# Pooling's mixing products moved between the token tiles of the last v chunk, their split moved to GpSimd

## The chip, the cores and the metric

The kernel is one program on one core of a Trainium2 chip. The metric is device time in microseconds: the median of three executions. One further execution was taken with the hardware profiler, and every row below comes from it. Engines are named as the profile names them: PE is TensorE, DVE is VectorE, ACT is ScalarE, POOL is GpSimd, SP issues DMAs.

## What is computed

Two blocks follow each other on 256 tokens of width 1024. The first, a two-layer transformer block with a context of 256 more tokens, holds the change. In each of its layers a projection makes u, q, k and v; u goes through a pooling mixer and q, k, v through differential attention, and both results side by side go through `w_out`:

```
u, q, k, v = split_heads(h @ w_in[l])
...
y = jnp.stack([centred_mean(g, w) - g for g, w in zip(groups, POOL_WINDOWS)], axis=2)
y = jnp.einsum('bngc,gcd->bngd', y, w_pool).reshape(b, n, POOL_WIDTH)
return y * s_pool
...
s = jnp.einsum('bhqd,bhkd->bhqk', q, k).astype(jnp.float32) * (HEAD_DIM ** -0.5)
a = jax.nn.softmax(s, axis=-1).reshape(b, N_HEADS, 2, nq, nk)
w = a[:, :, 0] - lam * a[:, :, 1]
return jnp.einsum('bhqk,bhkd->bhqd', w.astype(v.dtype), v)
...
mix = jnp.concatenate([pool_mixer(u, w_pool[l], s_pool[l]), head_out(o_att, g_subln[l], lam_init)], axis=-1)
x = x + ga * (mix @ w_out[l])
```

There are four pooling groups of 128 channels. The einsum with `w_pool` is what the code calls a mixing product, or mix. Layer 0 works on 512 tokens (context and latent), layer 1 attends over 512 keys but needs its results for 256 tokens only. The second block (another attention, a recurrence, feed-forward parts) is not touched.

## The kernel before

All large matrix products are made of three products each, because weights and activations are held as a rounded high part and a low remainder: `w_hi` and `w_lo`, `h_hi` and `h_lo`. Weights come in chunks of 1 MB, numbered through the whole program (`N_WIN[l]` is the first chunk of layer l's input projection, `N_WOUT[l]` the first of its output projection). For a chunk, ACT makes `w_hi` (`split_hi`), and DVE, or for a few chunks POOL (`weight_lo`), makes `w_lo`, each in two halves.

The engines run without a scheduler: each has its own instruction stream in the order in which the code is written, and semaphores tie the streams together. So a waiting instruction holds up everything behind it on its engine.

The input projection of a layer has eight chunks, c = 0 to 7. The last, c = 7, holds half of v and is computed by `gemm_t` in four token tiles of 128 tokens, 24 products each, one after the other. Its result lies in PSUM banks 2 and 3; DVE copies it to `v_tok` and then counts `psum_free` up. `score(l, 0)`, the scores of the first attention unit, stands before c = 7, and DVE and ACT make that unit's weights while c = 7 runs.

Attention follows, in units: 16 in layer 0 (the first eight over 512 keys, the other eight over 256), 8 in layer 1 (all over 512 keys). For a unit i, PE makes `score(l, i)`, two products (L798); DVE finds the maxima (L2001) and scales them (`maxima`, L2003); ACT exponentiates (L1438); DVE takes the reciprocals of the sums (L2012), a small factor (L2014) and the weights `wgt` from the two halves of `prob` (`weights`, L2018); PE transposes `wgt` into bank 0 (L810); ACT copies that to `wgtT` (L1446, `copyT`); PE multiplies by `v_tok` (`values`, L820). PE's stream in a unit is transposes(i), score(i + 3), values(i). Banks for scores alternate over 4-5, 6-7 and 2-3, so `score(l, 2)` has to wait until c = 7 has been copied out of banks 2 and 3.

Pooling sits in between. POOL makes `pool_y` from u during the projection (`centred`). The four mixes (`pool_mix`, L788) are issued by PE at the start of attention, mingled with scores 1 and 2; ACT writes their rounded high part to `h_hi` (`pool_hi`, L1429), DVE the remainder to `h_lo` (`pool_lo`, L1993). In banks 1, 4, 5 and 1 (`MIX_BANK`) these results lie where later scores and values go, so PE waits for `po_lo` three times:

```
pe.wait_ge(po_lo, 4 * l + 1)
pool_mix(l, 3)
pe.wait_ge(po_lo, 4 * l + 3)
...
if i == 0:
    pe.wait_ge(po_lo, 4 * l + 4)
```

POOL's part at that time is `weight_lo(N_WOUT[l] + 1, ...)`, two instructions on 128x1024 elements. `h_hi` and `h_lo` are also the operands of c = 7, so nothing may be written to them before c = 7 ends.

Of the kernel before, what the change touches and what calls it, by code (L numbers as in the profile page):

```python
# [99 lines left out]
def build_program(nc, w_stream, w_ada, x_in, vec_in, cst_in, pool_inv, gla_masks, gla_sums, w_pool, w_gk, w_gk2,  # L100
                  out):
    ctx = ExitStack()
    with ctx:
# [116 lines left out]
        def sem(name):  # L220
# [27 lines left out]
        y_ready, po_done, po_hi, po_lo = (  # L248
            sem("y_ready"), sem("po_done"), sem("po_hi"), sem("po_lo"))
# [92 lines left out]
        MIX_BANK = (1, 4, 5, 1)  # L342
# [72 lines left out]
        def _(pool):  # L415
# [48 lines left out]

            for i in range(ADA_WIN):
# [7 lines left out]
                if i in (3, 5, 7, 9):  # L473
                    centred(0, (i - 3) // 2)
            weight_lo(N_WOUT[0] + 1, 0)
# [23 lines left out]
            for g in range(4):  # L499
                centred(1, g)  # L500
            weight_lo(N_WOUT[1] + 1, 0)
# [47 lines left out]
        def _(pe):  # L549
# [123 lines left out]
            def gemm_t(n, tiles, ready=None, bank=None, free=None, middle=None):  # L673
# [6 lines left out]
                for i in range(tiles):  # L680
# [10 lines left out]
                    if i == 0 and middle is not None:  # L691
                        middle()
                last.then_inc(gemm_done, 1)
# [90 lines left out]
            def pool_mix(l, g):  # L784

                w = ALLT if l == 0 else SEQ
                pe.wait_ge(y_ready, 4 * l + g + 1)
                mm(ps[:, MIX_BANK[g], 0:w], wp[:, l, g, :], pool_y[:, g, 0:w], start=True, stop=True).then_inc(po_done, 1)  # L788

# [12 lines left out]
            def attention(units, u0, q0, l):  # L802
# [51 lines left out]
                if l == 0:  # L854
                    ada_columns(4, 4)
                transposes(0)
                pe.wait_ge(pool_in, 32)
                pool_mix(l, 0)
                pool_mix(l, 1)
                pe.wait_ge(ada_ready, 3 + 6 * l)  # L860
                score(l, 1)
                pool_mix(l, 2)
                pe.wait_ge(psum_free, N_WIN[l] + 8)
                score(l, 2)
                pe.wait_ge(po_lo, 4 * l + 1)
                pool_mix(l, 3)
                pe.wait_ge(po_lo, 4 * l + 3)
                for i in range(count):
# [118 lines left out]
            for l in range(2):  # L987
                n0 = N_WIN[l]
                hr = (h_ready, H0[f"win{l}"])
                for c in range(8):  # L990
# [5 lines left out]
                    elif c < 6:  # L996
                        gemm_f(n, h_hi, h_lo, slice(0, ALLT if l == 0 else SEQ), None, bank=bank, free=free)
                    else:
                        gemm_t(n, 4, bank=bank, free=free)
# [331 lines left out]
        def _(act):  # L1331
# [93 lines left out]
            def pool_hi(l, g):  # L1425
# [1444 lines left out]
```

## Time and profile before

| what | value |
|---|---|
| runs, median (lowest to highest) | 1576.99 us (1576.82 to 1578.64) |
| the profiled execution's own time | 1578.42 us |
| span of its records | 1576.6 us |
| PE busy | 1550.2 us, 98% |
| DVE busy | 1102.3 us, 70% |
| ACT busy | 744.1 us, 47% |
| POOL busy | 162.4 us, 10% |
| mean granted clock of TensorE | 0.995 |
| c = 7 of layer 0 ends, its attention begins | at 134.8 us of the span |
| c = 7 of layer 1 ends, its attention begins | at 676.6 us of the span |

Times inside the run are microseconds from the start of the span. A line of a timeline gives when a group of like instructions started and how long it took, and in brackets how long the engine had been idle and for whom it waited. A mean clock of 1.00 is 2.4 GHz, 0.50 is 1.2 GHz. Two fp32 products of this kernel are two records of PE each, so a count x4 stands for two products.

### The profile page before, as it was taken

The numbers are of one execution on the slowest core, as the hardware profiler recorded it, in microseconds if no ns is written. First come the engines' busy times: TensorE is split into PE (matmuls) and PEld (weight loads), VectorE is DVE, ScalarE is ACT, GpSimd is POOL, SyncE is SP. The second block draws the span as 40 slices with busy tenths as digits, with TensorE's granted clock in tenths as the row PEclk, the third lists the DMA queues.
The fourth block names the chain that finished last, engine by engine and source line by source line (L and its number), as shares of the span: only waits on it lengthen the run. The fifth ranks groups of instructions, "written<-read, shape, count | busy, mean of one in ns | idle before, by whom it ended". The sixth has DMA issues, their size and how long they took to land.

```text
span 1576.6 us, 27327 instructions
## 1 busy us (share of the span) xinstructions
PE 1550.2 (98%) x11138; PEld 1403.2 (89%) x11138; DVE 1102.3 (70%) x1674; ACT 744.1 (47%) x1064; POOL 162.4 (10%) x151
## 2 busy tenths in 40 slices
PE   9999999999999999999999999999999999999998
PEld 6786777888888887978999999999999999999998
DVE  5676658555565666867666678668786889887786
ACT  4215534222231323355444465667464567665554
POOL 0341100000000000410000010201020211021110
PEclk9999999999999999999999999999999999999999
DMA  9861453432343432415544543335455445545541
GB/s 391 327 239 58 175 198 110 159 108 105 134 159 122 144 117 84 171 69 194 191 180 162 211 159 108 117 138 178 183 187 188 161 164 184 188 161 205 178 181 52
DMA packets 36525, 257.76 MB, mean 163 GB/s; under 512 B 4087, under 2 KB 4088, under 8 KB 5968
## 3 DMA queue, kind: packets, MB, share of 16 engines
q1 hardware_dynamic: 29952, 211.85, 37.0%
q0 software_dynamic: 6480, 44.58, 7.4%
q8 instruction: 69, 1.13, 0.3%
q14 instruction: 24, 0.20, 0.0%
HBM read 255.37 MB, written 1.05 MB: 163 GB/s over the span
## 4 chain that ended last, share of the span: by engine, by line
PE 87%; DVE 6%; ACT 4%; issue 2%; DMA 2%; SPq 0%; DVEq 0%; ACTq 0%
PE ps L578 17%; PE ps L580 17%; PE ps L579 17%; PE ps L616 4%; PE ps L615 4%; PE ps L614 4%; PE ps L702 1%; PE ps L686 1%; PE ps L595 1%; PE ps L820 1%; PE ps L597 1%; PE ps L596 1%; PE ps L687 1%; PE ps L688 1%; DVE w_lo L1866 1%
## 5 line engine op out<-in xcount | busy, mean ns | idle before, releaser
L1351 ACT ACTIVATE w_hi<-w_raw 128x1024 fp32r<-128x1024 f32 x378 | 395.7, 1056 | 526.6 <-PE ps L580 300.7
L1866 DVE TENSOR_TENSOR w_lo<-w_raw,w_hi 128x1024 fp32r<-128x1024 f32 x375 | 468.4, 1253 | 142.0 <-ACT w_hi L1351 138.5
L578 PE MATMUL ps<-h_hi,w_hi 128*128 128x256 f32 (+1 forms) x1616 | 496.0, 307 | 0.7 <-DVE h_lo L1919 0.3
L580 PE MATMUL ps<-h_hi,w_lo 128*128 128x256 f32 (+1 forms) x1616 | 493.1, 305 | 0.0
L579 PE MATMUL ps<-h_lo,w_hi 128*128 128x256 f32 (+1 forms) x1616 | 493.0, 305 | 0.0
L578 PEld LDWEIGHTS ps<-h_hi,w_hi 128*128 128x128 f32 x1616 | 308.7, 191 | 18.0 <-issue 2.7
L580 PEld LDWEIGHTS ps<-h_hi,w_lo 128*128 128x128 f32 x1616 | 308.7, 191 | 13.4
L579 PEld LDWEIGHTS ps<-h_lo,w_hi 128*128 128x128 f32 x1616 | 308.8, 191 | 12.8
L614 PE MATMUL ps<-g_hi,w_hi 128*128 128x256 f32 (+1 forms) x448 | 140.4, 313 | 0.0
L615 PE MATMUL ps<-g_lo,w_hi 128*128 128x256 f32 (+1 forms) x448 | 140.4, 313 | 0.0
L616 PE MATMUL ps<-g_hi,w_lo 128*128 128x256 f32 (+1 forms) x448 | 140.4, 313 | 0.0
L2087 DVE SCALAR_TENSOR_TENSOR x<-ps,ada,x 128x256 f32<-128x256 f32 x120 | 50.9, 477 | 90.2 <-PE ps L616 60.3
L578 PE MATMUL ps<-g_hi,w_hi 128*128 128x256 f32 (+1 forms) x368 | 111.4, 303 | 0.0
L580 PE MATMUL ps<-g_hi,w_lo 128*128 128x256 f32 (+1 forms) x368 | 111.0, 302 | 0.0
L579 PE MATMUL ps<-g_lo,w_hi 128*128 128x256 f32 (+1 forms) x368 | 110.9, 301 | 0.0
L2568 DVE SCALAR_TENSOR_TENSOR conv_y<-ffn_s,vec,conv_y 128x255 f32<-128x255 f32 x192 | 95.6, 539 | 7.6 <-ACT conv_y L1744 5.7
L614 PEld LDWEIGHTS ps<-g_hi,w_hi 128*128 128x128 f32 x448 | 85.5, 191 | 5.0
L615 PEld LDWEIGHTS ps<-g_lo,w_hi 128*128 128x128 f32 x448 | 85.5, 191 | 5.0
L616 PEld LDWEIGHTS ps<-g_hi,w_lo 128*128 128x128 f32 x448 | 85.5, 191 | 5.0
L2334 DVE TENSOR_TENSOR relu<-relu 128x1024 f32<-128x1024 f32 (+1 forms) x32 | 30.7, 959 | 69.7 <-ACT relu L1565 69.7
L580 PEld LDWEIGHTS ps<-g_hi,w_lo 128*128 128x128 f32 x368 | 70.4, 191 | 2.6
L579 PEld LDWEIGHTS ps<-g_lo,w_hi 128*128 128x128 f32 x368 | 70.4, 191 | 2.4
(375 smaller groups left out, 2505.0 us busy)
## 6 DMA issues: line engine op xcount, KB each, us to landing
w_raw<-in_w_stream SPq DMA_DIRECT2D x188, 1024.0 KB, 4.8
ada_r<-in_w_ada POOLq DMA_DIRECT2D x20, 1024.0 KB, 5.2
ada_g<-in_w_ada POOLq DMA_DIRECT2D x16, 1024.0 KB, 7.5
ada_r<-in_w_ada SPq DMA_DIRECT2D x4, 1024.0 KB, 14.2
ada_g<-in_w_ada SPq DMA_DIRECT2D x4, 1024.0 KB, 22.8
ada_s<-in_w_ada POOLq DMA_DIRECT2D x4, 1024.0 KB, 5.2
x<-in_x_in SPq DMA_DIRECT2D x2, 1024.0 KB, 6.2
w_raw<-in_w_stream SPq DMA_DIRECT2D x4, 512.0 KB, 18.4
```

Source lines behind the costliest of these rows:

```text
L578: mm(o, wh, hi[:, k, cols], start=(k == 0), stop=False)
L579: mm(o, wh, lo[:, k, cols], start=False, stop=False)
L580: last = mm(o, wl, hi[:, k, cols], start=False, stop=(k == KT - 1))
L595: mm(o, wh, hi[:, k, cols], start=(k == 0), stop=False)
L614: mm(o, wh, hi[:, k, cols], start=(k == 0), stop=False)
L615: mm(o, wh, lo[:, k, cols], start=False, stop=False)
L616: last = mm(o, wl, hi[:, k, cols], start=False, stop=(k == KT - 1))
L1351: A(w_hi[:, n % 2, k, :].rearrange("p k n -> p (k n)"), w_raw[:, n % 4, k.start * CH:k.stop * CH], ACT.Copy)\
L1866: TT(w_lo[:, n % 2, k, :].rearrange("p k n -> p (k n)"), w_raw[:, n % 4, k.start * CH:k.stop * CH], w_hi[:, n % 2, k, :].rearrange("p k n ...
L2087: last = STT(x[:, t, c], ps[:, bank + m, c], ada[:, l, part + t, s:s + 1], x[:, t, c], ALU.mult, ALU.add)
L2334: TT(relu2[:, :, 0:w], relu[:, c % 2, :, 0:w], relu[:, c % 2, :, 0:w], ALU.mult)\
L2568: last = STT(y, ffn_s[:, t, 0:SEQ - back], V(f"ffn{l}", o), y, ALU.mult, ALU.add)
```

## The change

In both layers the same things are moved. PE: the four mixes leave the start of attention and go behind the first token tile of c = 7 (mixes 0 and 1, in layer 0 also `ada_columns(4, 4)`) and behind the second (mixes 2 and 3); `score(l, 1)` and the transposes of unit 0 go behind the third. The waits of PE for `po_lo` at the start of attention are gone; one remains before the first product of `w_out`. Mixes now lie in banks 7, 1, 0 and 7. ACT: the two-step split is replaced by one plain copy of each mix into `pool_y` (`mixed_copy`), ahead of the exponentials of unit 1; those and `copyT` of unit 0 now stand ahead of the `split_hi` that follows c = 7. POOL: `mixed_split` waits until c = 7 has ended, then makes `h_hi` by a copy and `h_lo` by a subtraction for each group, and only then comes its `weight_lo`. DVE: the four `pool_lo` are gone, and `maxima(l, 1)` (and `ada_columns` in layer 0) go ahead of the copy of v. ACT's copies of `o_raw`, which lies over `pool_y`, wait for `po_lo`.

```diff
-        MIX_BANK = (1, 4, 5, 1)
+        MIX_BANK = (7, 1, 0, 7)
...
+            def mixed_split(l):
+
+                w = ALLT if l == 0 else SEQ
+                pool.wait_ge(gemm_done, N_WIN[l] + 8)
+                for g in range(4):
+                    pool.wait_ge(po_copied, 4 * l + g + 1)
+                    own.step(nc.gpsimd.tensor_copy(h_hi[:, g, 0:w], pool_y[:, g, 0:w]))
+                    own.join()
+                    PT(h_lo[:, g, 0:w], pool_y[:, g, 0:w], h_hi[:, g, 0:w].bitcast(F32), ALU.subtract).then_inc(po_lo, 1)
...
+            mixed_split(0)
...
+            mixed_split(1)
...
+                    if i in between:
+                        between[i]()
...
             def pool_mix(l, g):
                 w = ALLT if l == 0 else SEQ
+                if l == 0 and g == 0:
+                    pe.wait_ge(pool_in, 32)
+                if g == 1:
+                    pe.wait_ge(psum_free, N_WIN[l] + 7)
+                if g == 3:
+                    pe.wait_ge(po_copied, 4 * l + 1)
                 pe.wait_ge(y_ready, 4 * l + g + 1)
                 mm(ps[:, MIX_BANK[g], 0:w], wp[:, l, g, :], pool_y[:, g, 0:w], start=True, stop=True).then_inc(po_done, 1)
+
+            def mixes(l, pair):
+
+                if l == 0 and pair == 0:
+                    ada_columns(4, 4)
+                pool_mix(l, 2 * pair)
+                pool_mix(l, 2 * pair + 1)
+
+            def first_units(l):
+
+                u, kb = 16 * l, (ALLT - UNITS[l][0][2]) // P
+                pe.wait_ge(po_copied, 4 * l + 4)
+                pe.wait_ge(ada_ready, 3 + 6 * l)
+                score(l, 1)
+                pe.wait_ge(wgt_ready, u + 1)
+                for b in range(kb):
+                    last = nc.tensor.transpose(ps[:, 0, b * P:(b + 1) * P], wgt[:, u % 2, b * P:(b + 1) * P], ident)
+                last.then_inc(wgtT_done, 1)
...
-                if l == 0:
-                    ada_columns(4, 4)
-                transposes(0)
-                pe.wait_ge(pool_in, 32)
-                pool_mix(l, 0)
-                pool_mix(l, 1)
-                pe.wait_ge(ada_ready, 3 + 6 * l)
-                score(l, 1)
-                pool_mix(l, 2)
                 pe.wait_ge(psum_free, N_WIN[l] + 8)
                 score(l, 2)
-                pe.wait_ge(po_lo, 4 * l + 1)
-                pool_mix(l, 3)
-                pe.wait_ge(po_lo, 4 * l + 3)
...
+                            pe.wait_ge(po_lo, 4 * l + 4)
...
-                    if i == 0:
-                        pe.wait_ge(po_lo, 4 * l + 4)
...
+                        gemm_t(n, 4, bank=bank, free=free,
+                               between={0: lambda: mixes(l, 0), 1: lambda: mixes(l, 1), 2: lambda: first_units(l)})
...
-            def pool_hi(l, g):
+            def mixed_copy(l, g):
                 w = ALLT if l == 0 else SEQ
                 act.wait_ge(po_done, 4 * l + g + 1)
-                A(h_hi[:, g, 0:w], ps[:, MIX_BANK[g], 0:w], ACT.Copy, scale=V(f"s_pool{l}", g)).then_inc(po_hi, 1)
+                A(pool_y[:, g, 0:w], ps[:, MIX_BANK[g], 0:w], ACT.Copy, scale=V(f"s_pool{l}", g)).then_inc(po_copied, 1)
...
+                    act.wait_ge(po_lo, q + 1)
...
-                copyT(0)
-                pool_hi(l, 0)
-                pool_hi(l, 1)
-                exponentials(l, 1)
-                pool_hi(l, 2)
-                pool_hi(l, 3)
...
+                        for g in range(4):
+                            mixed_copy(l, g)
+                        exponentials(l, 1)
+                        copyT(UNITS[l], 16 * l, 0)
...
-            def pool_lo(l, g):
-
-                w = ALLT if l == 0 else SEQ
-                dve.wait_ge(po_hi, 4 * l + g + 1)
-                STT(h_lo[:, g, 0:w], ps[:, MIX_BANK[g], 0:w], V(f"s_pool{l}", g), h_hi[:, g, 0:w].bitcast(F32),
-                    ALU.mult, ALU.subtract).then_inc(po_lo, 1)
...
-                pool_lo(l, 0)
-                maxima(l, 1)
-                pool_lo(l, 1)
-                pool_lo(l, 2)
                 weights(l, 1)
-                pool_lo(l, 3)
...
                     else:
                         maxima(l, 0)
                         weights(l, 0)
+                        if l == 0:
+                            ada_columns(0, 4, 4, 32)
+                        maxima(l, 1)
```

PE's stream in layer 0, from the last product of c = 7 on, before (`cst,rows` is `ada_columns`, `cst,wgt` are transposes, `pool_y,wp` mixes, `kT,qT` scores, `v_tok,wgtT` values):

```order
L713 MATMUL ps<-cst,rows 128x8 x2
L810 MATMUL ps<-cst,wgt 128x128 x4
L788 MATMUL ps<-pool_y,wp 128x512 x2
L798 MATMUL ps<-kT,qT 128x512 x2
L788 MATMUL ps<-pool_y,wp 128x512
L798 MATMUL ps<-kT,qT 128x512 x2
L788 MATMUL ps<-pool_y,wp 128x512
L798 MATMUL ps<-kT,qT 128x512 x2
L820 MATMUL ps<-v_tok,wgtT 128x128 x4
```

PE's stream in layer 0 now; the rows with `h_hi,w_hi`, `h_lo,w_hi` and `h_hi,w_lo` are products of c = 7, and 24 of them stand between two of the inserted pieces:

```order
L727 MATMUL ps<-cst,rows 128x8 x2
L808 MATMUL ps<-pool_y,wp 128x512 x2
L698 MATMUL ps<-w_hi,h_hi 128x256
...
L700 MATMUL ps<-w_lo,h_hi 128x256
L808 MATMUL ps<-pool_y,wp 128x512 x2
L698 MATMUL ps<-w_hi,h_hi 128x256
...
L836 MATMUL ps<-kT,qT 128x512 x2
L825 MATMUL ps<-cst,wgt 128x128 x4
L698 MATMUL ps<-w_hi,h_hi 128x256
...
L700 MATMUL ps<-w_lo,h_hi 128x256
L836 MATMUL ps<-kT,qT 128x512 x4
L858 MATMUL ps<-v_tok,wgtT 128x128 x4
L848 MATMUL ps<-cst,wgt 128x128 x4
L836 MATMUL ps<-kT,qT 128x512 x2
```

All four mixes, one score and one set of transposes stand between products of c = 7, and behind its last product two scores and the values of unit 0 come at once.

POOL's stream in layer 0 from the end of `centred` on, before (two DMAs of other weights, then `weight_lo`):

```order
L462 TENSOR_TENSOR pool_y<-win_sum,u_pad 128x512
L468 DMA ada_g_72<-in_w_ada 128x2048
L468 DMA ada_g_73<-in_w_ada 128x2048
L428 TENSOR_TENSOR w_lo<-w_raw,w_hi 128x1024 x2
L481 DMA ada_r_68<-in_w_ada 128x2048
```

and now:

```order
L478 DMA ada_g_73<-in_w_ada 128x2048
L471 CAST h_hi<-pool_y 128x512
L473 TENSOR_TENSOR h_lo<-pool_y,h_hi 128x512
...
L471 CAST h_hi<-pool_y 128x512
L473 TENSOR_TENSOR h_lo<-pool_y,h_hi 128x512
L428 TENSOR_TENSOR w_lo<-w_raw,w_hi 128x1024 x2
L492 DMA ada_r_68<-in_w_ada 128x2048
```

Eight instructions on 128x512 elements have come between those DMAs and `weight_lo`; in layer 1 the same eight work on 128x256.

## Rows read from the trace of the kernel before

**Rows 1.** The page: busy time, share of the span and instructions of each engine.

```profile
PE 1550.2 (98%) x11138; PEld 1403.2 (89%) x11138; DVE 1102.3 (70%) x1674; ACT 744.1 (47%) x1064; POOL 162.4 (10%) x151
```

**Rows 2.** Windows: stretch, length, busy of PE PEld DVE ACT POOL, TensorE clock, DMA, GB/s.

```profile
144.00:150.00 6.00, 5.35 (x27) 3.66 (x26) 5.35 (x10) 3.27 (x9) 0.00 (x0) 0.72 0.00 0
676.00:690.00 14.00, 11.51 (x54) 6.81 (x53) 10.49 (x18) 8.21 (x20) 4.67 (x2) 0.88 0.20 76
```

**Rows 3.** Timeline of PE, layer 0: start, us, engine, line, operation, count, [idle before].

```profile
134.80 0.51 PE L713 MATMUL ps<-cst,rows 128*128 128x8 f32 x4
135.16 0.63 PE L810 MATMUL ps<-cst,wgt 128*128 128x128 f32 x4
135.63 1.88 PE L788 MATMUL ps<-pool_y,wp 128*128 128x512 f32 x4
137.45 1.13 PE L798 MATMUL ps<-kT,qT 64*128 64x512 f32 x4
...
142.95 1.13 PE L798 MATMUL ps<-kT,qT 64*128 64x512 f32 x4 [1.21 <-DVE h_lo L1993]
144.73 1.64 PE L820 MATMUL ps<-v_tok,wgtT 128*128 128x128 f32 x8 [0.65 <-DVE h_lo L1993]
...
149.93 0.60 PE L810 MATMUL ps<-cst,wgt 128*128 128x128 f32 x4
```

**Rows 4.** Timeline of PE, layer 1, the same columns.

```profile
676.60 0.60 PE L810 MATMUL ps<-cst,wgt 128*128 128x128 f32 x4
677.03 1.03 PE L788 MATMUL ps<-pool_y,wp 128*128 128x256 f32 x4
...
683.74 1.32 PE L798 MATMUL ps<-kT,qT 64*128 64x512 f32 x4 [2.30 <-DVE h_lo L1993]
...
690.12 0.60 PE L810 MATMUL ps<-cst,wgt 128*128 128x128 f32 x4
```

**Rows 5.** Timeline of DVE and PE in one unit of layer 1.

```profile
689.24 1.22 DVE L2001 TENSOR_REDUCE small<-ps 128x2 f32<-128x1024 f32 x1
...
690.50 0.17 DVE L2003 TENSOR_SCALAR small<-small 128x2 f32<-128x2 f32 x1
...
690.65 1.13 PE L798 MATMUL ps<-kT,qT 64*128 64x512 f32 x4
...
691.11 0.75 DVE L2018 SCALAR_TENSOR_TENSOR wgt<-prob,small 128x512 f32<-128x512 f32 x1
...
691.71 1.16 PE L820 MATMUL ps<-v_tok,wgtT 128*128 128x128 f32 x8
...
692.71 0.49 PE L810 MATMUL ps<-cst,wgt 128*128 128x128 f32 x3
```

**Rows 6.** Timeline of DVE, layer 0: the copy of the last v chunk.

```profile
135.00 1.23 DVE L2240 COPY v_tok<-ps 128x1024 f32<-128x1024 f32 x1 [7.03 <-PE ps L688]
```

**Rows 7.** Timeline of POOL, then its groups by form (busy us, mean ns).

```profile
60.08 1.30 POOL L462 TENSOR_TENSOR pool_y<-win_sum,u_pad 128x512 f32<-128x512 f32 x1
...
69.90 1.06 POOL L456 TENSOR_TENSOR win_sum<-u_pad 128x516 f32<-128x516 f32 x1
...
656.53 0.74 POOL L462 TENSOR_TENSOR pool_y<-win_sum,u_pad 128x256 f32<-128x256 f32 x1
...
L511 POOL MEMSET gq<- 128x1024 f32 x1 | 1.0, 957 | 20.2 <-DVE x L2087 20.2
```

**Rows 8.** Timeline of POOL and DVE where both work at once.

```profile
86.61 1.29 POOL L460 TENSOR_TENSOR win_sum<-win_sum,p_inv 128x512 f32<-128x512 f32 x1
...
86.67 1.78 DVE L1983 TENSOR_TENSOR qT<-qT,rope_tmp 128x512 f32<-128x512 f32 x1
...
87.98 1.63 POOL L462 TENSOR_TENSOR pool_y<-win_sum,u_pad 128x512 f32<-128x512 f32 x1
...
676.62 4.67 POOL L428 TENSOR_TENSOR w_lo<-w_raw,w_hi 128x1024 fp32r<-128x1024 f32 x2 [13.40 <-ACT w_hi L1351]
...
680.43 0.89 DVE L2003 TENSOR_SCALAR small<-small 128x2 f32<-128x2 f32 x1
```

More of the change, by code:

```diff
@@ L246, in build_program @@
         relu_ready, ghi_ready = sem("relu_ready"), sem("ghi_ready")
-        y_ready, po_done, po_hi, po_lo = (
-            sem("y_ready"), sem("po_done"), sem("po_hi"), sem("po_lo"))
+        y_ready, po_done, po_copied, po_lo = (
+            sem("y_ready"), sem("po_done"), sem("po_copied"), sem("po_lo"))
         qk_ready, pool_step = sem("qk_ready"), sem("pool_step")
@@ L671, in at_of, with gemm_t @@
                 return lambda k: ready[3] * ready[2] + (ready[1] + k)
-            def gemm_t(n, tiles, ready=None, bank=None, free=None, middle=None):
+            def gemm_t(n, tiles, ready=None, bank=None, free=None, middle=None, between=()):
                 start_chunk(n, same, free)
@@ L997, in _ @@
                         gemm_f(n, h_hi, h_lo, slice(0, ALLT if l == 0 else SEQ), None, bank=bank, free=free)
-                    else:
-                        gemm_t(n, 4, bank=bank, free=free)
+                    elif c == 6:
+                        gemm_t(n, 4, bank=bank, free=free)
+                    else:
+                        gemm_t(n, 4, bank=bank, free=free,
+                               between={0: lambda: mixes(l, 0), 1: lambda: mixes(l, 1), 2: lambda: first_units(l)})
                     if l == 0:
@@ L1423, in norm_split, with copyT @@
                         last.then_inc(norm_hi, 1)
-            def pool_hi(l, g):
+            def mixed_copy(l, g):
                 w = ALLT if l == 0 else SEQ
                 act.wait_ge(po_done, 4 * l + g + 1)
-                A(h_hi[:, g, 0:w], ps[:, MIX_BANK[g], 0:w], ACT.Copy, scale=V(f"s_pool{l}", g)).then_inc(po_hi, 1)
+                A(pool_y[:, g, 0:w], ps[:, MIX_BANK[g], 0:w], ACT.Copy, scale=V(f"s_pool{l}", g)).then_inc(po_copied, 1)
+            def copyT(units, u0, i):
+                u, w = u0 + i, ALLT - units[i][2]
+                act.wait_ge(wgtT_done, u + 1)
+                A(wgtT[:, u % 2, 0:w], ps[:, 0, 0:w], ACT.Copy).then_inc(wgtT_copied, 1)
             def exponentials(l, i):
@@ L1442, in attention @@
             def attention(units, u0, q0, l):
-                def copyT(i):
-                    u, w = u0 + i, ALLT - units[i][2]
-                    act.wait_ge(wgtT_done, u + 1)
-                    A(wgtT[:, u % 2, 0:w], ps[:, 0, 0:w], ACT.Copy).then_inc(wgtT_copied, 1)
                 def copy_o(q):
                     act.wait_ge(pv_done, u0 + 4 * (q - q0 + 1))
+                    act.wait_ge(po_lo, q + 1)
                     A(o_raw[:, q - q0, :], ps[:, 1, :], ACT.Copy).then_inc(o_copied, 1)
@@ L1477, in attention @@
                         A(sm(S_SQRT), sm(S_EPS), ACT.Sqrt)
-                    copyT(i)
+                    copyT(units, u0, i)
                     if i >= 4 and i % 4 == 0:
@@ L2249, in _ @@
                     if l == 0:
-                        if c in (3, 5, 7):
+                        if c in (3, 5):
                             ada_columns(0, (c + 1) // 2, 4, 4 * (c + 1))
```

## Prediction

> **What bounds the kernel now.** I read the page first: PE is busy for 98% of the span, DVE for 70%, POOL for 10% [rows 1]. So time can only be won in PE's idle and slow stretches, and at the start of attention there are both. I then went along PE's timeline in the two places. In layer 0 c = 7 ends at 134.80 and the transposes of unit 2 start at 149.93: 15.13 us, with two waits for `pool_lo` (1.21 and 0.65 us) [rows 3]. In layer 1 the same way goes from 676.60 to 690.12: 13.52 us, one wait of 2.30 [rows 4]. Last the windows: behind those waits the granted clock averages 0.72 over 6 us and 0.88 over 14 us, in both cases 3.4 us at the lower level (6 x 0.28 / 0.5 and 14 x 0.12 / 0.5) [rows 2]. The values of unit 0 take 1.64 us there, where the same eight records take 1.16 later [rows 3, 5].
>
> Behind that start PE takes 2.59 us for a unit: transposes at 690.12, score at 690.65, values at 691.71, the next transposes at 692.71, so 0.53, 1.06 and 1.00 [rows 4, 5]. DVE needs nearly as much: reduction to scaling 1.26 us, scaling to `wgt` 0.61, and 0.67 of `wgt`'s 0.75 (its end overlaps the next instruction), together 2.54 [rows 5]. PE is slower by 0.05 us a unit. A DVE that falls behind therefore takes PE with it, and nothing later in the units gives it back.
>
> **The change on PE.** Layer 0, by the rows: columns 0.36, two mixes 1.82 and again 1.82, a score 1.06, transposes 0.47 now stand inside c = 7 [rows 3, 5]: c = 7 ends 5.53 us later, at 140.33. ACT's copy of each pair of mixes has a token tile of c = 7 to hide behind, and of that tile's 24 products none waits for it. Then a new wait: `score(l, 2)` needs the copy of v, which DVE starts 0.20 us after c = 7 and which takes 1.23 [rows 6]; with 0.03 that I add for signalling PE idles 1.46 us, where mixes and scores covered this before. Queued behind it is all of PE's attention. Then two scores, values, transposes, score, values: 3 x 1.06 + 2 x 1.00 + 0.53 = 5.71. Transposes of unit 2 start at 140.33 + 1.46 + 5.71 = 147.50, which is 2.43 us earlier than 149.93. Layer 1: the four mixes are half as wide and take 0.96 a pair (1.03 less the overlap of its end) [rows 4], so 1.92 + 1.06 + 0.43 = 3.4 go into c = 7, which ends at 680.0; with the same 7.17 behind it the transposes of unit 2 start at 687.17, 2.95 earlier. The sum without POOL: **5.4 us gained**. It counts the full clock in both places; one wait of 1.46 is shorter than the 1.86 in two parts and the 2.30 that were followed by the low one.
>
> **The change on ACT and DVE, outside that.** ACT writes each mix once as before. Exponentials of unit 1 and `copyT` of unit 0 now precede the `split_hi` after c = 7; ACT idles for long stretches in c = 7 and is through some 2 us after its end, before it is needed for unit 2. DVE loses four `pool_lo`. The w_raw transfer that waits for `weight_lo` starts later and is for a chunk that comes after attention. I cost these at nothing; the cover is ACT's idle time in c = 7 and the 16 or 8 units before `w_out`.
>
> **The change on POOL.** POOL has work in attention, and this is the term that decides. Before, its two `weight_lo` (4.67 us, 2.34 each, [rows 8]) ran from the end of c = 7 while DVE worked on PSUM results. Now eight instructions precede them, and all ten run beside the first units. What that does to DVE the trace shows: a DVE instruction with two SBUF inputs that meets a running POOL instruction ends only after it. L1983 started at 86.67 beside a POOL instruction that ended at 87.90, and took 1.78 us, where L2018 of the same size takes 0.75 alone; the next POOL instruction took 1.63 instead of 1.30 in its turn [rows 5, 7, 8]. Even the scaling of two numbers, L2003, took 0.89 instead of 0.17 at 680.43, and ended with `weight_lo` at 681.3 [rows 5, 8]. The stretch is the rest of POOL's instruction less about 0.14. L2003, L2018 and the small L2014 between them are of this kind in every unit; the reduction reads PSUM alone and isn't. The v copy beside a running `weight_lo` took its 1.23 too [rows 6].
>
> The Trainium skill, page "SBUF — State Buffer", section "Who interferes with whom", has it as a rule: GpSimd shares a pair of SBUF ports with VectorE, an instruction takes it whole, and VectorE instructions with two SBUF inputs or in a 2-port mode contend, while a reduction never does. The trace agrees in each case above. By it the ten instructions cost time; a reading that counts POOL as idle capacity gives the 5.4 us gain.
>
> Durations for POOL: subtraction 1.30 us in layer 0 and 0.74 in layer 1, `weight_lo` 2.34 [rows 7, 8]. The SBUF copy is not in the trace: at least half of a memset of twice the size, 0.48, at most an addition with two inputs, 1.06 [rows 7]. I take 0.6 (0.35 in layer 1), since with one input it is nearer to the memset. The page "GPSIMD Engine Reference" of the Trainium skill, section "Engine selection", calls one-input operations roughly line-rate, which as an estimate would be about 0.45 us for 512 elements and 0.6 with its dispatch; the sum would be the same.
>
> Now step by step, in us after c = 7 of layer 0. POOL: copy 0.1 to 0.7, subtraction to 2.1, copy to 2.8, and so on. DVE: v copy to 1.35, reciprocal, L2014 meets the first subtraction (0.40 lost), `wgt` of unit 1 the second copy (0.36); scaling for unit 2 the third copy (0.43); `wgt` of unit 2 the fourth subtraction (0.16 and 1.07); scaling for unit 4 the first `weight_lo` (0.74); L2014 of unit 3 the second (2.08). Together 5.2 us; `wgt` of unit 3 is ready at 14.5 instead of 9.3. DVE has 0.4 us in hand, so the transposes of unit 3 are 4.8 us late, in idle stretches of about 1.0, 1.0 and 2.8. Layer 1, with the shorter instructions: 0.5 at unit 1, 0.1, then 1.9 and 2.1 at the two `weight_lo`: 4.5, and the transposes of unit 2 are 3.9 late. So without the clock layer 0 gives -2.43 + 4.8 = +2.35, layer 1 -2.95 + 3.9 = +0.95. The idle stretches are as long as those that the low clock followed before. 3.4 us at half the clock cost at most half of that, 1.7 us; part would be hidden by DVE's lag, so I add 1.0 in each layer. **Sum: 2.35 + 0.95 + 2.0 = +5.3 us.** The span of 1576.6 becomes 1581.9. The profiled execution's own time was 1578.42, 1.8 around its span and 1.4 above the median of the runs; with the same distances it becomes 1583.7, and the median 1576.99 + 5.3 = 1582.3.
>
> Bounds: with the copy anywhere from 0.48 to 1.06 the meetings shift, for whether a DVE instruction meets the start or the end of one of 2.34 us is chance. Layer 0 then lies between +2.1 and +5, layer 1 between 0 and +3; together +2.5 to +8. After `weight_lo` has ended (13.6 us after c = 7) nothing of this goes on, and its result is needed only after the units.
>
> **Rivals.**
>
> *Hidden anyway: faster.* POOL's turns cost PE nothing, because the units have slack that I don't see, or L2014 and L2018 don't take turns. Then the whole -5.4 stands, 1571.6 (1571 to 1573.5). For it: no L2018 met POOL before, so its own row is missing. Against: two other instructions with two SBUF inputs, and L2003 itself, did. It decides if PE's idle time behind the v copy stays under 1 us a layer. 0.21.
>
> *Half of it.* The two `weight_lo` fall beside reductions and waits for ACT, and only the short turns cost: in layer 0 the first five, 2.4 us, instead of 5.2, in layer 1 0.6 instead of 4.5, with no fall of the clock. Less 0.4 in hand in each that is -2.43 + 2.0 and -2.95 + 0.2, so -3.2; with one of the four long turns met after all about -1, and with one and a low stretch +1. I call it -3 to +2.5, with 1576.5 in the middle. For it: a reduction is 1.2 of DVE's 2.54 us. Against: a DVE instruction that waits for one `weight_lo` is there when the next begins. 0.20.
>
> *Slower, as worked out.* +2.5 to +8, likeliest 1582.3, its own range 1579.5 to 1585. 0.59.
>
> **How the numbers follow.** 0.2% (3.15 us) is about what a measurement of this kernel can tell from no change. The slower case passes +3.15 in nine of ten: 0.53, and a little more for a stall unseen: 0.56. Within 0.2%: the rest of it and most of the half case, 0.23. Faster: the hidden case, 0.21. The range is 1572.5 to 1586: it takes in both bounds of the likeliest, the half case, and a part of the hidden one.
>
> **What would show it.** In the profile after: mixes, score and transposes between products of c = 7 with no idle time ahead of them; PE idle about 1.4 us before the score of unit 2; the instructions of L2018 (now L2038) above their 0.75 us, up to 1.8, and those of L2014 (now L2034) up to 2.3, while POOL runs; POOL busy for 13 to 15 us after c = 7 in layer 0, 10 in layer 1; transposes of unit 3 of layer 0 about 14.5 us after c = 7. I am wrong if L2038 keeps 0.75 beside POOL, or if the waits ahead of PE are short although they are stretched.

## The result and the profile after

The changed kernel takes 1583.66 us (median of 5 executions, 1582.24 to 1584.21) against 1576.82 of the kernel before beside it: 1.0044 times as long, 95% interval 1.0033 to 1.0055, so 5.2 to 8.7 us slower. The forecast was 1582.3 us, 5.3 more than before. One of the twelve executions of a kernel below, the one with `weight_lo` shortened, took 2520.9 us at a mean granted clock of 0.554; the other eleven took 1573.40 to 1578.16, with a median of 1575.79.

The span of the profiled execution is 1579.9 us, only 3.3 above that of before. The rest of it is at the start of the program, which the change doesn't touch: c = 7 of layer 0 begins at 120.75 here and began 2.4 us later before (the last section comes back to it). I therefore compare stretches, which start with the first product of c = 7 and end with the last `values` of the layer. In the timeline of PE of the changed kernel, these rows bound layer 0:

```profile
120.75 0.39 PE L698 MATMUL ps<-w_hi,h_hi 128*128 128x256 f32 x1
...
178.08 0.71 PE L858 MATMUL ps<-v_tok,wgtT 128*128 128x128 f32 x4 [0.16 <-ACT wgtT L1462]
```

That is 178.79 - 120.75 = 58.04 us. Read in the same way, in us (the median of before is the one beside each group of kernels, and the ratios below are to that one):

| kernel | median | layer 0 | layer 1 | both, against before |
|---|---|---|---|---|
| before | 1576.5 to 1577.1 | 55.41 | 39.90 | |
| changed | 1583.66 | 58.04 | 43.08 | +5.8 |
| weight_lo shortened | 1575.98 | 55.19 | 37.29 | -2.8 |
| split shortened | 1575.64 | 54.68 | 38.17 | -2.5 |
| both shortened | 1572.84 | 53.30 | 36.83 | -5.2 |
| before, weight_lo shortened | 1575.90 | 54.93 | 38.61 | -1.8 |
| pieces behind reductions | 1575.22 | 55.30 | 37.37 | -2.6 |
| filler, too long | 1583.11 | 58.06 | 42.46 | +5.2 |
| filler, half | 1581.69 | 58.01 | 40.72 | +3.4 |
| weight_lo on VectorE | 1582.69 | 60.22 | 40.21 | +5.1 |
| split inside c = 7, pieces | 1572.57 | 53.42 | 36.84 | -5.1 |
| the same, weight_lo at once | 1581.78 | 56.98 | 42.83 | +4.5 |
| the same, pieces, two v copies | 1573.13 | 52.99 | 36.30 | -6.0 |

The stretches are read from one profiled execution of each kernel, and the medians don't agree with them in full: against before, each of the twelve kernels has a median 0.6 to 2.5 us higher than its stretches say. A part of this lies outside the span of the records: an execution's own time is longer than its span by 1.8 us in the kernel before, by 2.3 in the changed one and by 1.8 to 2.4 in the others. And the profiled execution of before had a low clock in both stretches [rows 2], which its others need not have had; there is no second trace of it. So against before the stretches make every kernel look better than its median does, by 1.2 us on average.

Now the stretch itself. The timeline of PE in the changed kernel answers to [rows 3, 4], layer 0 first, layer 1 from 681.73 on: L836 is the score, L848 the transposes, L858 the values.

```profile
137.76 0.28 PE L700 MATMUL ps<-w_lo,h_hi 128*128 128x256 f32 x1
139.35 1.99 PE L836 MATMUL ps<-kT,qT 64*128 64x512 f32 x8 [1.32 <-DVE v_tok L2258]
...
144.89 1.16 PE L858 MATMUL ps<-v_tok,wgtT 128*128 128x128 f32 x8 [0.96 <-ACT wgtT L1462]
146.71 1.07 PE L848 MATMUL ps<-cst,wgt 128*128 128x128 f32 x4 [0.66 <-DVE wgt L2038]
147.71 2.08 PE L836 MATMUL ps<-kT,qT 64*128 64x512 f32 x4
...
152.09 0.66 PE L848 MATMUL ps<-cst,wgt 128*128 128x128 f32 x4 [0.99 <-DVE wgt L2038]
...
681.73 1.99 PE L836 MATMUL ps<-kT,qT 64*128 64x512 f32 x8 [1.32 <-DVE v_tok L2258]
...
686.83 1.16 PE L858 MATMUL ps<-v_tok,wgtT 128*128 128x128 f32 x8 [0.53 <-ACT wgtT L1462]
691.12 1.11 PE L848 MATMUL ps<-cst,wgt 128*128 128x128 f32 x4 [3.14 <-DVE wgt L2038]
692.17 2.08 PE L836 MATMUL ps<-kT,qT 64*128 64x512 f32 x4
...
696.04 0.76 PE L848 MATMUL ps<-cst,wgt 128*128 128x128 f32 x4
```

The mixes are inside c = 7 without a wait, and the first score behind it waits 1.32 us for the v copy. The waits for `po_lo` are gone. In their place PE waits for `wgt` and `wgtT`: 0.96, 0.66 and 0.99 us in layer 0 and 0.53 and 3.14 in layer 1. From 146.71 and from 691.12 the same records take almost twice as long (1.07 and 2.08 us for 0.60 and 1.13). Why `wgt` is late stands in DVE's timeline, first of layer 0 and from 682.08 on of layer 1 (L2023 is the scaling, L2034 the small factor, L2038 `wgt`):

```profile
139.41 0.67 DVE L2034 SCALAR_TENSOR_TENSOR small<-small 128x1 f32<-128x1 f32 x1
140.12 1.05 DVE L2038 SCALAR_TENSOR_TENSOR wgt<-prob,small 128x512 f32<-128x512 f32 x1
...
142.34 0.54 DVE L2023 TENSOR_SCALAR small<-small 128x2 f32<-128x2 f32 x1
...
144.91 1.74 DVE L2038 SCALAR_TENSOR_TENSOR wgt<-prob,small 128x512 f32<-128x512 f32 x1
146.57 1.21 DVE L2021 TENSOR_REDUCE small<-ps 128x2 f32<-128x1024 f32 x1
147.82 1.06 DVE L2023 TENSOR_SCALAR small<-small 128x2 f32<-128x2 f32 x1
...
148.99 2.19 DVE L2034 SCALAR_TENSOR_TENSOR small<-small 128x1 f32<-128x1 f32 x1
...
682.08 1.30 DVE L2038 SCALAR_TENSOR_TENSOR wgt<-prob,small 128x512 f32<-128x512 f32 x1
...
685.97 1.96 DVE L2023 TENSOR_SCALAR small<-small 128x2 f32<-128x2 f32 x1
...
688.03 2.18 DVE L2034 SCALAR_TENSOR_TENSOR small<-small 128x1 f32<-128x1 f32 x1
```

And POOL's timeline of the changed kernel beside it:

```profile
138.10 0.61 POOL L471 CAST h_hi<-pool_y 128x512 fp32r<-128x512 f32 x1 [31.05 <-PE ps L700]
138.80 1.26 POOL L473 TENSOR_TENSOR h_lo<-pool_y,h_hi 128x512 fp32r<-128x512 f32 x1
...
146.06 5.10 POOL L428 TENSOR_TENSOR w_lo<-w_raw,w_hi 128x1024 fp32r<-128x1024 f32 x2
...
685.55 4.65 POOL L428 TENSOR_TENSOR w_lo<-w_raw,w_hi 128x1024 fp32r<-128x1024 f32 x2
```

In layer 0 the small factor of unit 3, one number a partition, starts at 148.99, soon after the second `weight_lo` has begun, and ends at 151.18, when that instruction ends (146.06 + 5.10 = 151.16). The reduction, which reads PSUM, keeps its 1.21 us beside POOL. The windows of the changed kernel (length, busy times, then the TensorE clock as the third number from the end) show the low level in both layers:

```profile
144.00:150.00 6.00, 4.45 (x17) 2.44 (x18) 5.59 (x8) 3.85 (x11) 5.92 (x5) 0.73 0.00 0
...
685.00:699.00 14.00, 10.34 (x49) 6.39 (x48) 11.79 (x16) 7.11 (x20) 5.20 (x3) 0.76 0.21 75
```

By the working of the prediction that is 6 x 0.27 / 0.5 = 3.2 us at 1.2 GHz in layer 0, as before, and 14 x 0.24 / 0.5 = 6.7 in layer 1, twice as much as before [rows 2].

### The profile page after: what moved, and what is told of

Same layout as the page of the kernel before. It is cut to its first block, busy times and chain, and to the rows that moved or that the text cites. A ratio compares the mean times of both kernels' runs of the same rounds, so it can differ in the third digit from the quotient of the medians.

```text
span 1579.9 us, 27342 instructions
## 1 busy us (share of the span) xinstructions
PE 1548.2 (98%) x11138; PEld 1403.4 (89%) x11138; DVE 1106.1 (70%) x1666; ACT 744.1 (47%) x1064; POOL 175.1 (11%) x167
## 3 DMA queue, kind: packets, MB, share of 16 engines
q8 instruction: 69, 1.13, 0.3%
## 4 chain that ended last, share of the span: by engine, by line
PE 86%; DVE 8%; ACT 3%; issue 2%; DMA 1%; SPq 0%; DVEq 0%; ACTq 0%
PE ps L590 17%; PE ps L591 17%; PE ps L592 17%; PE ps L628 4%; PE ps L627 4%; PE ps L626 4%; PE ps L716 1%; PE ps L698 1%; PE ps L607 1%; PE ps L609 1%; PE ps L608 1%; PE ps L700 1%; PE ps L699 1%; DVE w_lo L1893 1%; DMA ada_r<-in_w_ada 1%
```

## The experiments

My theory, called port theory below: a VectorE instruction with two SBUF inputs, or a scaling, that meets a running GpSimd instruction waits for it, and what waits for VectorE is PE; a low clock comes on top. Rivals: the new wait for the v copy is the cost, GpSimd's work costs wherever it stands, or the number of its instructions does.

**GpSimd's work cut away, one part at a time.** Three kernels from the changed one. The first leaves out all but 8 columns of each `weight_lo` of this chunk, the second all but 8 columns of each instruction of the split, the third both.

```diff
-                PT(w_lo[...], w_raw[...], w_hi[...], ALU.subtract)
+                e = 8 if cut else 1024
+                PT(w_lo[...][:, 0:e], w_raw[...][..., 0:e], w_hi[...][:, 0:e], ALU.subtract)
```
```diff
             def mixed_split(l):
-                w = ALLT if l == 0 else SEQ
+                w = 8
```

> The changed kernel with GpSimd's two weight_lo of each attention cut to 8 of their 1024 columns (the rest of that low part is left out), mixed_split as it is. Port theory (VectorE instructions with two SBUF inputs, or the scaling, wait for the running GpSimd instruction): in the changed kernel two VectorE instructions met each weight_lo pair, 1.06 + 2.19 us in layer 0 and 1.96 + 2.18 in layer 1 where 0.17 + 0.22 are normal. Without them 2.86 and 3.75 us go, and with layer 1's low clock behind its 3.14 us wait another 2 to 2.5: attention of both layers together 7 to 9 us shorter than in the changed kernel, so 1575 to 1577.5 us, with waits of about 1 us for the short turns still in layer 0. Rival, the new wait for the v copy (1.32 us) and the low clock after it are the cost and GpSimd's turns lie in slack: within 2 us of the changed kernel, 1582 to 1585.

> The changed kernel with mixed_split cut to 8 columns a piece (the split of the mixes is left out but for these), weight_lo as it is. It is short work then, so weight_lo starts about 1 us after the end of c = 7, when ScalarE has made w_hi, and ends near 5.7 us after it. Port theory: the long turns are still met by VectorE, now in unit 1 (small factor or weights, scaling), up to 2.2 us each; the short ones (0.45 + 0.30 + 0.37 + 0.99 us in layer 0, 0.04 + 0.55 + 0.09 in layer 1) are gone. Worked out along the stream: layer 0 1.5 us shorter than in the changed kernel, layer 1 0.5, low clock about as before: 1580 to 1583. Rival, it is the number of GpSimd instructions (each handover costs) that matters: eight of ten are gone, and 4 to 5 of the 5.8 us should go, 1577.5 to 1579.

> The changed kernel with both cut: no GpSimd instruction of length beside the units, all of the rest of the change there (mixes in c = 7, the wait for the v copy, ScalarE's and VectorE's new order). Port theory: what the prediction called the sum without POOL, -2.4 in layer 0 and -2.95 in layer 1 against the kernel before: 1570.5 to 1572.5 us, transposes of unit 2 7.2 us after the end of c = 7, no low clock. Rival, the wait for the v copy or the order of ScalarE and VectorE costs by itself: above 1575, with waits ahead of the transposes of units 1 to 3 and instructions at their normal lengths.

`weight_lo` shortened: 1575.98 us (ratio to before 0.9993, 0.9984 to 1.0001), as expected: the two stretches are 8.6 us shorter than in the changed kernel, where 7 to 9 were forecast. Both shortened: 1572.84 (0.9969, 0.9959 to 0.9980), 0.3 above the forecast range. Its stretches are 11.0 us shorter than those of the changed kernel, and this is its PE in layer 0 (L837 is the score, L859 the values, L849 the transposes):

```profile
140.73 1.99 PE L837 MATMUL ps<-kT,qT 64*128 64x512 f32 x8 [1.32 <-DVE v_tok L2259]
142.65 1.16 PE L859 MATMUL ps<-v_tok,wgtT 128*128 128x128 f32 x8
143.64 0.60 PE L849 MATMUL ps<-cst,wgt 128*128 128x128 f32 x4
...
146.35 0.60 PE L849 MATMUL ps<-cst,wgt 128*128 128x128 f32 x4
```

The wait for the v copy is there with its full 1.32 us, and nothing else is: the transposes of unit 2 start 6.9 us after c = 7 has ended at 139.41. So the rival with the v copy is dead, and so is one that blames the new order on ACT or DVE.

The shortened split missed its forecast: 1575.64 us (0.9989, 0.9980 to 0.9998), not 1580 to 1583. It is below the rival's 1577.5 to 1579 too. DVE's timeline of this kernel shows what I had wrong:

```profile
141.10 0.75 DVE L2038 SCALAR_TENSOR_TENSOR wgt<-prob,small 128x512 f32<-128x512 f32 x1
141.97 1.23 DVE L2021 TENSOR_REDUCE small<-ps 128x2 f32<-128x1024 f32 x1
143.23 0.86 DVE L2023 TENSOR_SCALAR small<-small 128x2 f32<-128x2 f32 x1
144.00 1.21 DVE L2021 TENSOR_REDUCE small<-ps 128x2 f32<-128x1024 f32 x1
145.25 1.14 DVE L2023 TENSOR_SCALAR small<-small 128x2 f32<-128x2 f32 x1
```

Its POOL:

```profile
141.23 5.13 POOL L428 TENSOR_TENSOR w_lo<-w_raw,w_hi 128x1024 fp32r<-128x1024 f32 x2
```

Eight short instructions still take 1.7 us, so `weight_lo` starts 1.8 us after c = 7 and not 1.0. By then `wgt` of unit 1 is under way, and the two long instructions fall on two reductions. Only the tails meet the scalings: 0.69 + 0.97 = 1.66 us lost, where the same two instructions took 2.86 in the changed kernel. That `weight_lo` and split give back 8.6 and 8.3 us each alone and 11.0 together fits this: what a long instruction costs depends on where it falls. All three numbers also contain the low clock, which is gone in each of these kernels (1.00 in both attentions).

**Was it the same before?** The kernel before with its `weight_lo` shortened in the same way.

> The kernel before with its two weight_lo of each attention cut to 8 columns (the rest of that low part left out). Port theory: there they ran 134.8 to 139.5 and 676.6 to 681.3, beside pool_lo and the v copy that read PSUM, and met only one scaling (0.89 for 0.17 us): 0 to 1.5 us a layer at most, of which a low stretch of the clock could be a part: 1575 to 1577. Rival, weight_lo costs about 4 us a layer wherever it stands at the start of attention (for what waits for it, not for the port): 1568 to 1571.

1575.90 us (0.9993, 0.9984 to 1.0001), stretches 1.8 us shorter in both layers together, and no low clock in them. It lies inside the forecast, far from the rival's 1568 to 1571: the same two instructions cost 1.8 us at their old place and 8.6 at the new one, the low clock included in both cases.

**The phase, turned both ways.** If the meeting costs and not the work, then the same work costs nothing behind reductions. From the changed kernel, with four pieces of 128x512 for the two of 128x1024:

```diff
             mixed_split(0)
-            weight_lo(N_WOUT[0] + 1, 0)
-            weight_lo(N_WOUT[0] + 1, 1)
+            for piece in range(4):
+                pool.wait_ge(wgt_ready, 3 + piece)
+                weight_lo_piece(N_WOUT[0] + 1, piece)
```

> The changed kernel, complete, with each weight_lo cut in two (four pieces of 128x512, about 1.27 us each), and each piece made to wait for the weights of units 2, 3, 4, 5 (wgt_ready), so that it starts when VectorE begins a reduction of 1.22 us, which reads PSUM alone. GpSimd does the same work. Port theory: what costs is not the work but the meeting; with the long turns behind reductions the kernel comes to where the one with the shortened weight_lo is, within 1.5 us: 1575 to 1577.5. Rival, GpSimd's traffic slows VectorE or ScalarE whatever they do: a good part of the 7 us between the two stays, 1579 to 1583, with longer reductions.

1575.22 us (0.9991, 0.9982 to 1.0000), and the stretches are 8.4 us shorter than in the changed kernel. With nothing left out it is where the shortened one was. POOL and DVE of this kernel, layer 0 (L2034 is the reduction here, L2036 the scaling, L2051 `wgt`):

```profile
149.49 1.27 POOL L438 TENSOR_TENSOR w_lo<-w_raw,w_hi 128x512 fp32r<-128x512 f32 x1 [1.28 <-DVE wgt L2051]
152.04 1.27 POOL L438 TENSOR_TENSOR w_lo<-w_raw,w_hi 128x512 fp32r<-128x512 f32 x1 [1.28 <-DVE wgt L2051]
```

```profile
149.33 1.22 DVE L2034 TENSOR_REDUCE small<-ps 128x2 f32<-128x1024 f32 x1
150.58 0.20 DVE L2036 TENSOR_SCALAR small<-small 128x2 f32<-128x2 f32 x1
...
151.20 0.75 DVE L2051 SCALAR_TENSOR_TENSOR wgt<-prob,small 128x512 f32<-128x512 f32 x1
```

A piece runs 149.49 to 150.76 beside a reduction; the scaling loses 0.03 us and `wgt` nothing. Beside all eight pieces, four in each layer, the scaling takes 0.20 to 0.22 us for 0.17. GpSimd has twelve instructions in each attention here, where the changed kernel has ten, so their number is not what costs either.

The other direction is in the last kernel of this part. It starts from the complete version below, whose GpSimd has no split to make before `weight_lo`, and has `weight_lo` uncut and at once:

```diff
-                pool.wait_ge(wgt_ready, u + 2)
-                weight_lo_piece(n, 0)
...
+                weight_lo(n, 0)
+                weight_lo(n, 1)
```

> The complete version with the split inside c = 7, but weight_lo uncut and without the wait for a reduction: two instructions of 2.34 us as soon as ScalarE has made w_hi, from about 1.0 to 5.7 us after c = 7. Port theory by the stream: VectorE's small factor of unit 1 comes at 1.5 us and waits for the first (1.8 us lost), the weights of unit 1 wait for the second (2.0 lost); VectorE has 0.4 us in hand, so 3.4 us a layer and a stretch of low clock behind it: 7 to 9 us above the version with the pieces, 1579 to 1582, above the kernel before although GpSimd has less to do than in it or in the changed one. Rival, the shortened split showed that two long turns without the short ones cost little (2.5 us below the kernel before in the two attentions): 1574 to 1576.

1581.78 us (1.0033, 1.0022 to 1.0044), as forecast, slower than before although POOL does less than in the changed kernel. DVE, layer 0:

```profile
140.90 2.08 DVE L2060 SCALAR_TENSOR_TENSOR small<-small 128x1 f32<-128x1 f32 x1
143.01 2.80 DVE L2064 SCALAR_TENSOR_TENSOR wgt<-prob,small 128x512 f32<-128x512 f32 x1
```

2.08 and 2.80 for 0.22 and 0.75: 1.86 and 2.05 us lost to the two instructions, which ran from 140.61 to 145.26. 9.6 us lie between this kernel's stretches and those of the version with the pieces, where 7 to 9 were forecast.

**The clock.** Products of the unit matrix into a part of bank 1 that nothing uses yet, ahead of PE's waits, so that only its idle time is filled. First with these counts, then with about half of them (4; 2 or 11; 3; 2):

```diff
+                filler(8)
                 pe.wait_ge(psum_free, N_WIN[l] + 8)
...
+                        filler({2: (5, 20)[l], 3: (7, 0)[l]}.get(i, 0))
                         transposes(i)
...
+                    filler(4 if i == 1 else 0)
                     values(i)
```

> The changed kernel with products of the unit matrix into a free part of bank 1 ahead of TensorE's waits (8 before the wait for the v copy, 4 before values 1, 5 or 20 before transposes 2, 7 before transposes 3 of layer 0), each set shorter than the wait. Waits stay the same length; only TensorE's idle time is filled. If the low clock (3.4 us in layer 0, 6.8 in layer 1) follows the idle stretches and costs 0.6 and 2.5 us of the changed kernel's 5.8, it is gone and the time is 1580 to 1581.5, transposes of unit 3 of layer 1 2.6 us after those of unit 2. Rival, the low clock costs nothing because VectorE's lag hides it, or comes from elsewhere: 1583 to 1584.

> The filler again, with half as many products, since one took 0.24 us and the first sets (1.95, 1.16, 1.28, 1.73, 4.63 us) overran the waits and made units late by up to 1.9 us themselves. Now 4 before the v copy's wait, 2 before values 1, 2 or 11 before transposes 2, 3 before transposes 3 of layer 0: 1.0, 0.5, 0.5 or 2.7, 0.7 us, each shorter than its wait. If the low clock costs 0.6 us in layer 0 and 2.4 in layer 1, the transposes of unit 2 start when they do in the changed kernel (25.8 us after c = 7 begins in layer 1), those of unit 3 2.6 us later instead of 4.9, and the time is 3 us below that of the changed kernel: 1580 to 1581.5. Rival, no gain from the clock: 1583 to 1584.

The first set missed its forecast: 1583.11 us (1.0040, 1.0027 to 1.0054), in the rival's range. It can't decide for the rival, because the filler overran the waits: in layer 1 the transposes of unit 2 start 27.70 us after c = 7 begins, 1.9 later than in the changed kernel. With half of it: 1581.69 us (1.0041, 1.0028 to 1.0055), 0.2 above the forecast range. PE of that kernel in layer 1 (L864 is the filler):

```profile
687.56 2.62 PE L864 MATMUL ps<-cst 128*128 128x128 f32 x22
690.87 0.66 PE L848 MATMUL ps<-cst,wgt 128*128 128x128 f32 x4 [0.69 <-DVE wgt L2045]
...
693.51 0.60 PE L848 MATMUL ps<-cst,wgt 128*128 128x128 f32 x4
```

The transposes of unit 2 start 25.84 us after c = 7 begins, as in the changed kernel (25.83), but the next follow after 2.64 us where it took 696.04 - 691.12 = 4.92. No clock fell in attention here: it is 1.00 in every window. Stretch by stretch the low clock cost 58.04 - 58.01 = 0.0 us in layer 0 and 43.08 - 40.72 = 2.4 in layer 1. The medians alone don't show it, since the two intervals overlap.

What makes the clock fall is not shown by this. PE's waits alone don't decide it: the kernel with `weight_lo` shortened has the changed kernel's three waits in layer 0, of the same length and at the same distance from c = 7 (1.32, 0.97 and 0.65 us), and its clock stays at 1.00. This is its transposes record of unit 2, where the changed kernel has 1.07 us:

```profile
146.60 0.65 PE L849 MATMUL ps<-cst,wgt 128*128 128x128 f32 x4 [0.65 <-DVE wgt L2039]
```

**weight_lo on VectorE.** VectorE needs 1.2 us for what takes GpSimd 2.34. From the changed kernel, with the two calls taken from GpSimd:

```diff
                 weights(l, 1)
+                split_lo(N_WOUT[l] + 1)
                 for i in range(len(units)):
```

> The changed kernel with the two weight_lo taken from GpSimd and made by VectorE after the weights of unit 1 (1.25 us each instead of 2.34), mixed_split as it is. Port theory: 8.6 us go for the long turns (what the shortened weight_lo gave in the two attentions), 2.5 us come back in each for VectorE's own work, less 0.4 that it has in hand: -8.6 + 4.2 = -4.4 against the changed kernel: 1578 to 1580.5. Rival, VectorE is so near to being the bound that its own work costs more than the turns did: 1583 or more.

1582.69 us (1.0039, 1.0025 to 1.0052): missed by 2.2 us, and just below the rival's 1583. Layer 1 did better than the forecast (+0.3 against before), layer 0 much worse (+4.8). DVE, POOL and PE of this kernel in layer 0:

```profile
142.50 3.83 DVE L1889 TENSOR_TENSOR w_lo<-w_raw,w_hi 128x1024 fp32r<-128x1024 f32 x2
```

```profile
143.65 1.60 POOL L471 CAST h_hi<-pool_y 128x512 fp32r<-128x512 f32 x1
145.33 2.12 POOL L473 TENSOR_TENSOR h_lo<-pool_y,h_hi 128x512 fp32r<-128x512 f32 x1
```

```profile
150.06 2.07 PE L854 MATMUL ps<-v_tok,wgtT 128*128 128x128 f32 x8 [4.72 <-ACT wgtT L1458]
```

The subtraction of `w_lo` has two SBUF inputs itself and took turns with the split: 3.83 us instead of some 2.4, and POOL waited in its turn (1.60 for 0.61, 2.12 for 1.26). All of it stands ahead of the maxima of unit 2, so PE idled 4.72 us at one place, and 6.8 us of low clock followed. In layer 1 PE idled 3.44 us at the same place, and no low clock followed:

```profile
693.24 1.16 PE L854 MATMUL ps<-v_tok,wgtT 128*128 128x128 f32 x8 [3.44 <-ACT wgtT L1458]
```

The changed kernel's clock was low after a wait of 3.14 us in layer 1, so here too the length of the wait doesn't tell. My sum had counted VectorE's work and not its own turns.

**A version that beats both.** The mixes stay inside c = 7, and their split goes there too, for the tokens whose tile is done. ScalarE makes the high part, VectorE the low part. A semaphore counts the tiles of c = 7; GpSimd keeps what is left, piece by piece behind reductions:

```diff
                     if i in between:
+                        last.then_inc(tile_done, 1)
                         between[i]()
...
+            def mixed_hi(l):
+                w = 3 * P if l == 0 else SEQ
+                act.wait_ge(tile_done, (4, 6)[l])
+                act.wait_ge(po_copied, 4 * l + 4)
+                for g in range(4):
+                    A(h_hi[:, g, 0:w], pool_y[:, g, 0:w], ACT.Copy).then_inc(po_hi, 1)
...
+            def mixed_lo(l):
+                for g in range(4):
+                    dve.wait_ge(po_hi, 5 * l + g + 2)
+                    TT(h_lo[:, g, 0:w], pool_y[:, g, 0:w], h_hi[:, g, 0:w].bitcast(F32), ALU.subtract).then_inc(po_lo, 1)
...
+                pool.wait_ge(wgt_ready, u + 2)
+                weight_lo_piece(n, 0)
+                pool.wait_ge(nmax, u + 3)
+                weight_lo_piece(n, 1)
```

> A complete version: the mixes stay inside c = 7, but ScalarE makes their high part and VectorE the low part inside c = 7 as well, for the tokens whose tiles are done (384 of 512 in layer 0, all 256 in layer 1), VectorE being idle there for 9 and 5 us; GpSimd does only the low part of the last 128 tokens of layer 0 and the four pieces of weight_lo, each started when a reduction starts. Port theory: like the kernel with both shortened, 1571.5 to 1574, against 1577 before; the wait for the v copy stays 1.3 us. Rival, VectorE's subtractions come late and hold back the v copy, or ScalarE's added copies hold back the exponentials of unit 1: PE waits more than 1.5 us at the v copy and it is 1575 or more.

1572.57 us (0.9979, 0.9968 to 0.9989). Its stretches are within 0.15 us of those of the kernel with both cut away, so the split and `weight_lo` are hidden. Then the v copy, half of it inside c = 7:

```diff
+                        dve.wait_ge(tile_done, 3 * l + 3)
+                        CP(v_tok[:, 0:2, CH:2 * CH], ps[:, b, :].rearrange("p (t n) -> p t n", t=2))
...
-                        CP(v_tok[:, :, (c % 2) * CH:(c % 2 + 1) * CH], ps[:, b:b + 2, :]...)
+                            CP(v_tok[:, 2:4, CH:2 * CH], ps[:, b + 1, :].rearrange("p (t n) -> p t n", t=2))
```

> The kernel with the split inside c = 7, and the copy of v in two: the first bank (token tiles 0 and 1) is copied during c = 7, the second (128x512, 0.67 us) after it. The wait ahead of the score of unit 2 should fall from 1.32 to 0.75 us, and all of attention follows it: 0.56 us a layer, 1.1 us less than the kernel with one copy. Rival, the wait is not what attention follows (TensorE has slack behind it): no difference.

PE of this kernel:

```profile
140.34 1.99 PE L852 MATMUL ps<-kT,qT 64*128 64x512 f32 x8 [0.78 <-DVE v_tok L2306]
```

The wait fell from 1.32 to 0.78 us, and the two stretches became 0.43 and 0.54 us shorter, 1.0 where 1.1 was forecast. The medians don't show it: 1573.13 us (0.9974, 0.9965 to 0.9983), with overlapping intervals. So the gain of the second copy is shown in the stretches, not in the time. Both versions beat the kernel before, by 1.7 to 5.0 and 2.7 to 5.5 us (the intervals times 1577).

## Why the prediction was right

The direction, the mechanism and the size held. By its own steps:

*PE.* c = 7 was to end 5.53 and 3.4 us later. It lasts 17.29 and 15.13 us where it lasted 11.78, so 5.51 and 3.35. The new wait was put at 1.46 and is 1.32. The transposes of unit 2 were to start 7.17 us after c = 7 without POOL; with both parts shortened they do after 6.94 in both layers. These times count from the end of the last product; the prediction counted from where the next one would start, 0.16 us earlier, and by that the two are 1.48 and 7.10. The 5.4 us to gain are real: that kernel's stretches are 5.2 shorter than before, and its median 4.2 lower.

*POOL's turns.* This was the term that decided. Layer 0 was forecast as 0.40, 0.36, 0.43, 1.23, 0.74 and 2.08, together 5.2 us lost; the rows above give 0.45, 0.30, 0.37, 0.99, 0.89 and 1.97, together 5.0, at the same six instructions. Layer 1: 4.5 forecast (its own terms, 0.5, 0.1, 1.9 and 2.1, add up to 4.6), and 0.04 + 0.55 + 0.09 + 1.79 + 1.96 = 4.4 measured. The copy, not in the trace of before, takes 0.61 us, and 0.6 was assumed. The transposes of unit 3 of layer 0 start 14.05 us after c = 7 (14.5 forecast), those of unit 2 of layer 1 10.70 (11.1). The Trainium skill, page "SBUF — State Buffer", section "Who interferes with whom", says that whoever issues first gets the shared ports for the whole instruction and the other fully blocks. The traces agree: 2.08 and 2.80 us for instructions of 0.22 and 0.75.

*The clock.* Here the sum was right by luck. 1.0 us was added in each layer; it is 0.0 in layer 0 and 2.4 in layer 1, as the filler showed. In layer 0 the low stretch lay between units 2 and 3, where PE would have waited for `wgt` anyway. The idle stretches of 1.0, 1.0 and 2.8 us became 0.96, 0.66 and 0.99, with slow products in the place of the rest. In layer 1 it came after the long wait, 6.7 us of it instead of 3.4, when POOL was done and DVE had caught up: DVE waits for PE there (0.70 us ahead of the reduction at 694.29), so nothing hid it. The step "part would be hidden by DVE's lag, so I add 1.0 in each layer" should have asked, for each layer, whether the lag is before or behind the low clock. And that the clock would fall at all was argued from the length of the idle stretches alone, which by the kernels above doesn't decide it.

*The rest.* The stretches give +5.8 and the medians +6.8. Of the difference of 1.0, 0.5 lies outside the span, where the prediction took the same distance as before (1.8 us; it is 2.3). For the other 0.5, which is inside the interval, I have no row.

*The rivals.* "Hidden anyway" is wrong: L2038 took up to 1.74 us and L2034 up to 2.19 beside POOL. "Half of it" did not happen in this kernel. But the shortened split, at -2.5 in the stretches, shows that it was no empty case. There `weight_lo` started 1.76 us after c = 7 of layer 0 and VectorE lost 1.66 us to it; in the kernel with `weight_lo` at once it started after 1.08 us and VectorE lost 3.91.

## What to carry over

An engine with free time is not free capacity if it shares a port with one that PE waits for: cost each of its instructions by what it can meet, up to its whole length, and expect 2 us for a number that takes 0.2. If the work must stay there, cut it to the length of an instruction that doesn't contend and start it with that one: the same subtractions then cost 0.03 to 0.05 us each. And before work is moved out of a wait into another engine, look for the idle time nearest to it; here VectorE was idle for 8.9 us in c = 7 of layer 0 and 5.3 us in that of layer 1, the very chunks into which the mixes went.

## What was not expected of the hardware

In some executions the clock is low at places that no change touched, and 1.6 us a time go there. Between the end of attention of layer 0 and c = 7 of layer 1 the kernel before takes 486.4 us (178.59 to 664.98), as the changed one does. The kernel with pieces behind reductions takes 489.7 and the one with two v copies 488.1. Windows over the norm in between, first the version with one v copy, where the way takes 486.4 too:

```profile
590.00:604.00 14.00, 13.81 (x118) 9.64 (x117) 9.54 (x23) 5.21 (x11) 0.77 (x3) 1.00 0.40 140
```

The one with two v copies:

```profile
590.00:604.00 14.00, 14.00 (x112) 9.34 (x110) 6.98 (x17) 4.25 (x8) 0.76 (x3) 0.88 0.48 174
```

The one with pieces behind reductions:

```profile
590.00:604.00 14.00, 14.00 (x97) 9.00 (x99) 4.53 (x11) 3.33 (x6) 0.53 (x1) 0.76 0.46 164
```

3.4 and 6.7 us at 1.2 GHz, with PE busy for all of the 14 us. The start of the program differs in the same way: in the first 24 us the mean clock is 0.86 in the kernel before and 1.00 in the changed one. This explains why the spans of the first pair differ by 3.3 us and the stretches by 5.8, and probably the 2 to 4 us between executions of one kernel. The timed executions of one kernel point the same way: with pieces behind reductions the fastest of eleven took 1573.59 us at a mean clock of 1.000, the slowest 1577.59 at 0.996. What sets off these falls, with PE busy throughout, stays open. For a change of a few microseconds, stretches between two fixed instructions said more than the medians.
